# Reordering the routing stretch ahead of the expert loop in a two-layer SSM, Fourier and mixture-of-experts kernel

## Chip, cores and metric

One core of one Trainium2 chip. The metric is the device time of one execution in microseconds (us), given as the median of several runs.

## What is computed

Two layers over 256 image tokens and 256 context tokens of width 1024. Each layer normalises and modulates the tokens, mixes them (a bidirectional state-space scan and a 2-D Fourier mix, both gated), adds and normalises, and then applies a mixture of experts. The change touches only what stands at the head of the mixture of experts:

```python
def _moe(h, router_w, router_bias, w1, w3, w2, ws1, ws3, ws2):   # h: 512 tokens in layer 0, 256 in layer 1
    scores = jax.nn.sigmoid(h @ router_w)                        # 64 experts in 8 groups
    sel = scores + router_bias                                   # best 4 groups by their two best, then
    top_e = lax.top_k(sel, TOP_K)[1]                             # the 8 best experts of each token
    gate = take(scores, top_e); gate = gate / gate.sum() * 2.5
    ...                                                          # tokens sorted into blocks of one expert
    def body(acc, blk):
        tok, g, e = blk
        xb = h_pad[tok]
        hb = jax.nn.silu(xb @ w1[e]) * (xb @ w3[e])
        return acc.at[tok].add((hb @ w2[e]) * g[:, None]), None
    shared = (jax.nn.silu(h @ ws1) * (h @ ws3)) @ ws2            # one expert for all tokens
    return routed[:n_tok] + shared
```

## The kernel before

Everything is written out by hand for five engines, each with its own instruction list, tied by counting semaphores. All is f32. `l` is the layer (0 or 1) and `nt` its number of 128-token tiles: 4 in layer 0, 2 in layer 1. Each layer runs in three parts: the token mixer, the routing stretch, and the expert loop.

**The routing stretch.** For each tile, TensorE transposes the normalised tokens (`u2_transposes`, L959), ScalarE scales and copies them into `u2T` (L1352), and TensorE then forms the router's logits (`logits`, L970) and transposes the tokens back (L973); ScalarE takes the sigmoid (L1359) and copies the tokens for storing (L1361). The next tile's logits wait for both copies. In layer 0 the rows for the final gate (`g2_rows`, L1024) stand in between for the first two tiles. VectorE routes two tiles at a time (`route`, L1758 to L1787). Then TensorE counts the tokens of each expert (`count_tokens`, L1031 to L1034, psum bank 7). From the count VectorE makes the plan (`plan_steps`, L1806 on; `expert_list`, up to L1842; `place_experts`; `expert_row`, L1845 and L1847, which marks `blocks_ready`; `place_tokens`, L1872 to L1896).

Then `one_hot(i)` writes two lists for each tile: `onec` (the column of each slot, 128x512, L1901) and `onep` (its place in the block, 128x1024, L1903). GpSimd multiplies `onec` by the token's number (L2038). TensorE sums products of both (`slot_table`, L1047, 16 instructions a tile), ScalarE copies the sum (L1390), TensorE folds it (L1050), and VectorE's `slot_table` (L1919 to L1922) makes the tables of token numbers (`tblg`). `gates(i)` (L1908 to L1914) forms the eight gates of each token of tile i from `scores`; it is needed only after the loop.

**Shared work.** The shared expert is computed in the same stretch, in pieces: `shared_up(i)` (16 instructions of L980 for two tiles, so 8 for each), ScalarE's silu (L1367), VectorE's product (`shared_h`, L1792), two transposes (`shared_ht`, L986 and L987), VectorE's copy (`shared_ht`, L1796), `shared_down(i)` (eight instructions of L992) and ScalarE's copy (`shared_out`, L1373). Its weights lie in the buffers of the third expert, so SyncE may load that expert only when the last `shared_down` has ended (L583).

**The expert loop.** Each step takes three experts' weights, 3 MB each: two experts share a pair of half-filled blocks, block 0, and one fills block 1 alone. GpSimd gathers the tokens of a block from DRAM (`gather`, index copy L2056, indirect DMA L2060) into one of two buffers `xg`. TensorE transposes them (`x_transpose`, L1091), ScalarE (L1401) and VectorE (L1962) copy one half each, and TensorE runs `pair_up` (32 instructions of L1105) or `alone_up` (L980), the transposes, `pair_down` (L1134) or `alone_down` (L992). SyncE loads the next pair's up weights when `pair_up` is done (semaphore `up`, L587), and the down weights after the down products (L590).

**What starts the loop.** SyncE, GpSimd and the others wait for `blocks_ready` and read the number of steps from it. At the start SyncE loads the first pair (6 MB), then, after the last shared product, the third expert; in layer 0 it then issues the small parameters of layer 1 and two 2 MB pieces of its modulation weights, the second one when VectorE has copied the first token block (L474). The gathers wait for `tblg`, for the stored tokens, and for the semaphore `xt_tp`: gather i waits for i + 2, and TensorE adds 3 to it once when the token buffers are free. `x_transpose(0)` waits for the gather, for ScalarE's mark `xt_act` and for VectorE's mark `xt_dve`; VectorE gives its own after all of `gates`.

## Time and profile before

| | us |
|---|---|
| median of 3 runs | 2822.78 |
| lowest and highest run | 2819.46, 2827.2 |
| the profiled execution's own time | 2817.16 |
| its span, first to last instruction | 2815.2 |
| TensorE matmuls busy | 2556.5 (91%) |
| VectorE busy | 962.3 (34%) |
| ScalarE busy | 543.5 (19%) |
| GpSimd busy | 250.2 (9%) |
| mean of the DMA engines over the span | 264 GB/s |

The page cuts the span into 40 slices of 70 us. Three of its lines show the stages; each digit is a share in tenths:

```profile
PE   6999999999987999899999889999996899999994
...
PEclk8999999999999999999999989999998899999997
DMA  8764444444426999999999844764451799999983
```

The first 770 us are layer 0's mixer, the two stretches of nines in the DMA line are the two expert loops (about 910 to 1550 us and 2215 to 2750 us), and the short stretch before each is where tokens are routed. Times below are us from the span's start. The timelines name the source line of an instruction and, in brackets, how long its engine had been idle before it and what released it. PE is TensorE, DVE is VectorE, ACT is ScalarE, POOL is GpSimd, SPq is SyncE's DMA queue.

### The profile page before, as it was taken

The numbers are of one execution on the slowest core, as the hardware profiler recorded it, in microseconds if no ns is written. First come the engines' busy times: TensorE is split into PE (matmuls) and PEld (weight loads), VectorE is DVE, ScalarE is ACT, GpSimd is POOL, SyncE is SP. The second block draws the span as 40 slices with busy tenths as digits, with TensorE's granted clock in tenths as the row PEclk, the third lists the DMA queues.
The fourth block names the chain that finished last, engine by engine and source line by source line (L and its number), as shares of the span: only waits on it lengthen the run. The fifth ranks groups of instructions, "written<-read, shape, count | busy, mean of one in ns | idle before, by whom it ended". The sixth has DMA issues, their size and how long they took to land. (4 is left out here: it accounts for less than half of the span.)

```text
span 2815.2 us, 35251 instructions
## 1 busy us (share of the span) xinstructions
PE 2556.5 (91%) x11348; PEld 1622.4 (58%) x11348; DVE 962.3 (34%) x2249; ACT 543.5 (19%) x1210; POOL 250.2 (9%) x400
## 2 busy tenths in 40 slices
PE   6999999999987999899999889999996899999994
PEld 3878888787873343343333377878884333433431
DVE  1336624448165111111111474445616211111114
ACT  1223411334121111111111022224311111111110
POOL 0000000000002111111111000000000112111110
PEclk8999999999999999999999989999998899999997
DMA  8764444444426999999999844764451799999983
GB/s 291 243 203 153 150 144 140 135 150 146 150 83 234 407 406 410 410 403 398 410 410 380 323 136 124 239 198 144 141 165 63 312 398 391 392 399 390 382 354 139
DMA packets 293119, 742.43 MB, mean 264 GB/s; under 512 B 33176, under 2 KB 208416, under 8 KB 238240
## 3 DMA queue, kind: packets, MB, share of 16 engines
q1 hardware_dynamic: 264672, 665.59, 63.3%
q0 software_dynamic: 28352, 75.56, 6.9%
q8 instruction: 61, 1.00, 0.1%
q14 instruction: 34, 0.28, 0.0%
HBM read 734.60 MB, written 52.58 MB: 280 GB/s over the span
## 5 line engine op out<-in xcount | busy, mean ns | idle before, releaser
L747 PE MATMUL psum<-arena 128*128 128x256 f32 x1984 | 450.1, 386 | 8.9 <-ACT arena L1202 5.0
L1105 PE MATMUL psum<-arena 128*64 128x512 f32 x1472 | 360.8, 635 | 83.0 <-DMA arena<-in_w 83.0
L747 PEld LDWEIGHTS psum<-arena 128*128 128x128 f32 x1984 | 381.6, 194 | 65.6 <-issue 5.7
L980 PE MATMUL psum<-arena 128*128 128x512 f32 x832 | 375.3, 595 | 0.0
L1982 DVE COPY arena<-psum 128x512 f32<-128x512 f32 x92 | 63.6, 691 | 614.5 <-PE psum L992 310.3
L1105 PEld LDWEIGHTS psum<-arena 128*64 128x64 f32 x1472 | 112.4, 145 | 265.4 <-issue 259.8
L1418 ACT ACTIVATE arena<-psum 128x512 f32<-128x512 f32 x92 | 55.0, 598 | 1054.2 <-PE psum L992 591.9
L980 PEld LDWEIGHTS psum<-arena 128*128 128x128 f32 x832 | 152.4, 192 | 155.3 <-issue 155.3
L758 PE MATMUL psum<-arena 128*128 128x256 f32 (+1 forms) x1088 | 236.1, 375 | 5.0 <-ACT arena L1202 5.0
L758 PEld LDWEIGHTS psum<-arena 128*128 128x128 f32 x1088 | 202.4, 197 | 37.3 <-ACT arena L1202 5.2
L992 PE MATMUL psum<-arena 128*128 128x512 f32 x416 | 197.8, 619 | 5.8 <-DVE arena L1796 3.6
L1545 DVE SCALAR_TENSOR_TENSOR grow<-psum,par,grow 128x255 f32<-128x255 f32 (+1 forms) x304 | 136.1, 479 | 149.6 <-ACT grow L1261 144.0
L2082 POOL DMA_INDIRECT results<-arena,ids x92 | 92.8, 1008 | 920.5 <-DVE arena L1982 920.5
L907 PE MATMUL psum<-arena 128*128 128x256 f32 x768 | 173.2, 379 | 0.0
L1134 PE MATMUL psum<-arena 128*64 128x512 f32 x736 | 168.1, 599 | 0.0
L1979 DVE COPY arena<-psum 128x256 f32<-128x256 f32 x92 | 39.0, 424 | 369.0 <-PE psum L987 369.0
L907 PEld LDWEIGHTS psum<-arena 128*128 128x128 f32 x768 | 144.1, 190 | 23.0
L992 PEld LDWEIGHTS psum<-arena 128*128 128x128 f32 x416 | 76.8, 195 | 120.8 <-issue 115.5
L1091 PEld LDWEIGHTS psum<-cst,arena 128*128 128x128 f32 x736 | 94.9, 194 | 81.7 <-issue 57.5
L2032 POOL MEMSET arena<- 128x1024 f32 x4 | 3.7, 950 | 1371.1 <-DVE arena L1787 1371.1
L1091 PE MATMUL psum<-cst,arena 128*128 128x128 f32 x736 | 105.5, 288 | 21.7 <-DMA arena<-tokens,idg 20.9
L1134 PEld LDWEIGHTS psum<-arena 128*64 128x64 f32 x736 | 48.7, 136 | 113.8 <-issue 113.8
(305 smaller groups left out, 2476.9 us busy)
## 6 DMA issues: line engine op xcount, KB each, us to landing
arena<-in_w SPq DMA_DIRECT2D x414, 1024.0 KB, 14.7
arena<-in_w_in SPq DMA_DIRECT2D x92, 1024.0 KB, 5.2
arena<-in_w_ada SPq DMA_DIRECT2D x32, 1024.0 KB, 7.9
arena<-results POOLq DMA_DIRECT2D x12, 2048.0 KB, 9.5
arena<-in_w_br_ssm SPq DMA_DIRECT2D x24, 768.0 KB, 4.5
arena<-in_w_ada SPq DMA_DIRECT2D x8, 2048.0 KB, 15.2
arena<-cumulated SPq DMA_DIRECT2D x36, 384.0 KB, 4.2
arena<-in_w_br_four SPq DMA_DIRECT2D x12, 1024.0 KB, 5.2
```

The source lines that it names most:

```text
L747: last = mm(o[:, a, :], w[:, k, a * P:(a + 1) * P], rhs[:, k, :], start=k == 0, stop=k == ks - 1, skip_group_check=True)
L758: last = mm(o[:, a, 0:cols], lhs[:, k, a * P:(a + 1) * P], w[:, k, 0:cols], start=k == 0, stop=k == KD - 1, skip_group_check=True)
L907: last = mm(o[:, a, :], w[:, k, a * P:(a + 1) * P], rhs[:, k, :], start=k == 0, stop=k == KD - 1, skip_group_check=True)
L980: last = mm(o.rearrange("p (a n) -> p a n", a=2), lhs(k), w[:, k, :, :], start=k == 0, stop=k == KD - 1)
L992: last = mm(bank[5 + half][:, :], src[:, k, :], w[:, k, half * 512:(half + 1) * 512], start=k == 0, stop=k == 1)
L1091: last = tp(psum[:, 2 + k // 4, (k % 4) * P:(k % 4 + 1) * P], xg[b].rearrange("p (q k) -> p k q", k=KD)[:, k, :], ident)
L1105: last = mm(bank[0][c, :].rearrange("p (a n) -> p a n", a=2), xTe[0][:, k, c], w13[b][:, k, :, :], start=k == 0, stop=k == KD - 1)
L1134: last = mm(bank[5 + half][c, :], hT[0][:, k, c], w2s[b][:, k, half * 512:(half + 1) * 512], start=k == 0, stop=k == 1)
L1418: a_(ysb[b][:, 0:512], bank[5], ACT.Copy).then_inc(z["y_act"], 1)
L1545: i_ = V.scalar_tensor_tensor(dst, src[:, a * SEQ + lo + sh:a * SEQ + hi + sh], par[:, 60 + tap * 20 + ch:61 + tap * 20 + ch], dst, ALU.mu ...
L1982: V.tensor_copy(ysb[b][:, 512:1024], bank[6]).then_inc(z["y_dve"], 1)
L2082: gp.indirect_dma_start(scratch["y"][l], bass.IndirectOffsetOnAxis(ap=ids[:, q:q + 1], axis=0), ysb[b], None, bounds_check=last_row, oob_i ...
```

## The change

It keeps every computation and moves pieces of it.

- TensorE adds 3 to `xt_tp` right after the first two tiles (layer 0) or after both (layer 1), no longer after the last `shared_out`.
- In layer 0 the third tile's logits and the fourth tile's transposes stand in the middle of `shared_up(0)`; `shared_up(1)` is ahead of the count; `slot_table` is ahead of `shared_down(2)` and `shared_ht(3)`.
- In layer 1 the count stands in the middle of `shared_up(0)`, and `shared_ht(0)`, `shared_down(0)` and `shared_ht(1)` come after `experts_to_row`.
- VectorE multiplies `onec` by the token numbers itself, and GpSimd's four (two) multiplications and their semaphore `columns_numbered` go. In layer 0 `one_hot(0)` and `(1)` come ahead of `shared_h(2)`, and `one_hot(2)` and `(3)` ahead of `shared_h(3)`. In layer 1 the two `shared_h` and the first `shared_ht` move behind `place_experts`, the second one behind the lists.
- VectorE's `slot_table` comes ahead of all `gates` in layer 0; in layer 1 `gates(0)` stays ahead of it.
- ScalarE copies the table's sum ahead of `shared_out(2)`.
- The second block's first `x_transpose` stands in the middle of the first `pair_up`.

```diff
--- before.py
+++ after.py
@@ -386,7 +386,7 @@
         t_gr = stage("gate_rows_ready", 1, 0)
 
         names = ("u2_normed u2_transposed u2_ready logits routed counted placed rank_tp blocks_ready "
-                 "back_tp back_copied u2_stored0 u2_stored1 u2_stored2 u2_stored3 onehots columns_numbered table_sum table_copied table_folded "
+                 "back_tp back_copied u2_stored0 u2_stored1 u2_stored2 u2_stored3 onehots table_sum table_copied table_folded "
                  "router_in shared_in shared_up shared_sil shared_h shared_ht shared_htc shared_y shared_out "
                  "g2_diag g2_rows g2_ready scores").split()
 
@@ -993,13 +993,13 @@
                     return last
 
 
-                def shared_up(i):
+                def shared_up(i, between=None):
                     if i == 0:
                         pe.wait_ge(s["shared_in"], of(l, "shared_in", 48))
                         pe.wait_ge(s["g2_ready"], of(l, "g2_ready", nt // 2))
                     if i >= 2:
                         pe.wait_ge(s["shared_h"], of(l, "shared_h", i - 1))
-                    up(bank[i % 2], lambda k: u2T[:, k, i * P:(i + 1) * P], w13[2]).then_inc(s["shared_up"], 1)
+                    up(bank[i % 2], lambda k: u2T[:, k, i * P:(i + 1) * P], w13[2], between).then_inc(s["shared_up"], 1)
 
                 def shared_ht(i):
                     pe.wait_ge(s["shared_h"], of(l, "shared_h", i + 1))
@@ -1041,7 +1041,6 @@
                 def slot_table():
                     for i in range(nt):
                         pe.wait_ge(s["onehots"], of(l, "onehots", 2 * i + 2))
-                        pe.wait_ge(s["columns_numbered"], of(l, "columns_numbered", i + 1))
                         for j in range(TOPK):
                             c = slice(j % 2 * HALF, (j % 2 + 1) * HALF)
                             last = mm(bank[7][c, 0:P], onec[i][:, j, :], onep[i][:, j, :], start=i == 0 and j < 2, stop=i == nt - 1 and j >= 6)
@@ -1051,16 +1050,23 @@
 
                 if nt == 2:
                     g2_rows(0)
-                for i in range(nt):
+                for i in range(2):
                     u2_transposes(i)
-                    if nt == 4 and i < 2:
+                    if nt == 4:
                         g2_rows(i)
                     logits(i)
-                shared_up(0)
-                count_tokens()
-                shared_up(1)
-                shared_ht(0)
+                pe.sem_inc(z["xt_tp"], 3)
                 if nt == 4:
+                    def third_tile():
+                        logits(2)
+                        u2_transposes(3)
+
+                    u2_transposes(2)
+                    shared_up(0, third_tile)
+                    logits(3)
+                    shared_up(1)
+                    count_tokens()
+                    shared_ht(0)
                     shared_down(0)
                     shared_ht(1)
                     experts_to_row()
@@ -1068,17 +1074,22 @@
                     shared_up(2)
                     shared_up(3)
                     shared_ht(2)
+                    slot_table()
+                    shared_down(2)
+                    shared_ht(3)
                 else:
+                    shared_up(0, count_tokens)
+                    shared_up(1)
                     experts_to_row()
-                shared_down(nt - 2)
-                shared_ht(nt - 1)
-                slot_table()
+                    shared_ht(0)
+                    shared_down(0)
+                    shared_ht(1)
+                    slot_table()
                 shared_down(nt - 1)
 
                 pe.wait_ge(s["shared_out"], of(l, "shared_out", nt))
                 pe.sem_inc(z["down"], 3)
                 pe.sem_inc(z["up"], 2)
-                pe.sem_inc(z["xt_tp"], 3)
                 pe.sem_inc(z["ht_tp"], 2)
                 pe.wait_ge(s["blocks_ready"], of(l, "blocks_ready", 1))
                 n = pe.value_load(bexp[0:1, P:P + 1], min_val=1, max_val=STEPS)
@@ -1141,8 +1152,7 @@
                     down(hT[1], w2s[2]).then_inc(z["down"], 1)
 
                 x_transpose(0, 0, 1)
-                x_transpose(1, 1, 1)
-                pair_up(0, 1)
+                pair_up(0, 1, lambda: x_transpose(1, 1, 1))
                 with pe.Fori(0, STEPS // UNR) as ii:
                     for u in range(UNR):
                         i = ii * UNR + u
@@ -1385,9 +1395,12 @@
                     shared_out(1)
                     shared_silu(2)
                     shared_silu(3)
-                shared_out(nt - 2)
+                else:
+                    shared_out(0)
                 act.wait_ge(s["table_sum"], of(l, "table_sum", 1))
                 a_(tabT, bank[7][:, 0:P], ACT.Copy).then_inc(s["table_copied"], 1)
+                if nt == 4:
+                    shared_out(2)
                 shared_out(nt - 1)
                 act.wait_ge(s["g2_ready"], of(l, "g2_ready", nt // 2))
                 act.sem_inc(z["xt_act"], 1)
@@ -1898,8 +1911,10 @@
                 def one_hot(i):
                     if i == 0:
                         dve.wait_ge(s["g2_ready"], of(l, "g2_ready", nt // 2))
-                    V.tensor_tensor(onec[i], cst[:, C_STEP:C_STEP + HALF].unsqueeze(1).to_broadcast([P, TOPK, HALF]),
-                                    slotc[:, i, :].unsqueeze(2).to_broadcast([P, TOPK, HALF]), ALU.is_equal).then_inc(s["onehots"], 1)
+                    link(V.tensor_tensor(onec[i], cst[:, C_STEP:C_STEP + HALF].unsqueeze(1).to_broadcast([P, TOPK, HALF]),
+                                         slotc[:, i, :].unsqueeze(2).to_broadcast([P, TOPK, HALF]), ALU.is_equal))
+                    V.tensor_tensor(onec[i], onec[i], cst[:, C_TOK + i * TOPK:C_TOK + (i + 1) * TOPK].unsqueeze(2).to_broadcast([P, TOPK, HALF]),
+                                    ALU.mult).then_inc(s["onehots"], 1)
                     V.tensor_tensor(onep[i], cst[:, C_STEP:C_STEP + P].unsqueeze(1).to_broadcast([P, TOPK, P]),
                                     slotp[:, i, :].unsqueeze(2).to_broadcast([P, TOPK, P]), ALU.is_equal).then_inc(s["onehots"], 1)
 
@@ -1923,32 +1938,39 @@
 
                 for q in range(nt // 2):
                     route(q)
-                shared_h(0)
+                if nt == 4:
+                    shared_h(0)
                 plan_steps()
                 expert_list()
-                shared_h(1)
-                shared_ht(0)
-                place_experts()
                 if nt == 4:
+                    shared_h(1)
+                    shared_ht(0)
+                    place_experts()
                     shared_ht(1)
-                expert_row()
-                if nt == 2:
-                    shared_ht(1)
+                    expert_row()
+                else:
+                    place_experts()
+                    shared_h(0)
+                    expert_row()
+                    shared_h(1)
+                    shared_ht(0)
                 place_tokens()
-                if nt == 4:
-                    shared_h(2)
                 one_hot(0)
                 one_hot(1)
                 if nt == 4:
+                    shared_h(2)
+                    one_hot(2)
+                    one_hot(3)
                     shared_h(3)
                     shared_ht(2)
-                    one_hot(2)
-                    one_hot(3)
+                else:
+                    shared_ht(1)
+                    gates(0)
+                slot_table()
+                if nt == 4:
+                    gates(0)
                     shared_ht(3)
-                for i in range(nt // 2):
-                    gates(i)
-                slot_table()
-                for i in range(nt // 2, nt):
+                for i in range(1, nt):
                     gates(i)
                 dve.sem_inc(z["xt_dve"], 1)
                 dve.sem_inc(z["y_dve"], 1)
@@ -2033,10 +2055,6 @@
                 link(last)
                 for b in range(2):
                     gp.dma_start(first[:, b:b + 1], sent[:, b:b + 1]).then_inc(e_s[l][b], 16)
-                for i in range(nt):
-                    gp.wait_ge(s["onehots"], of(l, "onehots", 2 * i + 1))
-                    G.tensor_tensor(onec[i], onec[i], cst[:, C_TOK + i * TOPK:C_TOK + (i + 1) * TOPK].unsqueeze(2).to_broadcast([P, TOPK, HALF]),
-                                    ALU.mult).then_inc(s["columns_numbered"], 1)
                 gp.wait_ge(s["blocks_ready"], of(l, "blocks_ready", 1))
                 for i in range(nt):
                     gp.wait_ge(s[f"u2_stored{i}"], of(l, f"u2_stored{i}", 16))
```

## Rows read from the trace of the kernel before

**Rows 1.** Busy time by window, layer 0's loop: engines, clock, DMA share, GB/s

```profile
910.00:1010.00 100.00, 90.48 (x327) 37.49 (x328) 15.00 (x28) 10.30 (x21) 17.92 (x30) 0.93 1.00 411
```

**Rows 2.** Timeline of TensorE, layer 0: start, us, line, instructions [idle before <-releaser]

```profile
806.41 2.00 PE L970 MATMUL psum<-arena 128*128 128x64 f32 x16 [1.25 <-ACT arena L1352]
...
822.94 3.68 PE L970 MATMUL psum<-arena 128*128 128x64 f32 x16 [3.00 <-ACT arena L1352]
...
828.11 7.82 PE L980 MATMUL psum<-arena 128*128 128x512 f32 x16
...
848.31 3.70 PE L992 MATMUL psum<-arena 128*128 128x512 f32 x8 [2.16 <-DVE arena L1796]
...
875.75 3.71 PE L1047 MATMUL psum<-arena 128*64 128x128 f32 x64
...
893.49 1.97 PE L1091 MATMUL psum<-cst,arena 128*128 128x128 f32 x8 [9.73 <-DMA arena<-tokens,idg]
...
899.74 7.88 PE L1105 MATMUL psum<-arena 128*64 128x512 f32 x32
```

**Rows 3.** The chain that ended last, in order of time, layer 1: start, us, what

```profile
2195.45 6.39 DMA arena<-tokens,idg
...
2206.68 8.05 PE psum L1105 x32
```

**Rows 4.** Timeline of GpSimd, layer 0, then layer 1

```profile
886.13 1.11 POOL L2060 DMA_INDIRECT arena<-tokens,idg  x1 [1.97 <-PEq L1081]
...
2179.84 1.95 POOL L2038 TENSOR_TENSOR arena<-arena,cst 128x512 f32<-128x512 f32 x1 [19.43 <-DVE arena L1901]
...
2195.45 1.12 POOL L2060 DMA_INDIRECT arena<-tokens,idg  x1 [6.21 <-PEq L1081]
```

**Rows 5.** Timeline of VectorE, layer 0

```profile
816.45 0.81 DVE L1452 TENSOR_SCALAR arena<-xres,mv,rsq 128x1024 f32<-128x1024 f32 x1
...
827.01 0.29 DVE L1758 TENSOR_TENSOR arena<-arena 128x128 f32<-128x128 f32 x1 [2.98 <-ACT arena L1359]
...
839.04 0.22 DVE L1806 TENSOR_SCALAR arena<-psum 128x64 f32<-128x64 f32 x1 [2.17 <-PE psum L1034]
...
853.16 0.42 DVE L1872 TENSOR_SCALAR arena<-psum 128x256 f32<-128x256 f32 x1
...
864.28 0.42 DVE L1792 TENSOR_TENSOR arena<-arena,psum 128x256 f32<-128x256 f32 x1 [2.80 <-ACT arena L1367]
...
865.22 1.22 DVE L1903 TENSOR_TENSOR arena<-cst,arena 128x1024 f32<-128x1024 f32 x1
...
882.57 0.22 DVE L1919 TENSOR_SCALAR arena<-psum 128x64 f32<-128x64 f32 x1
...
888.82 0.24 DVE L1914 TENSOR_SCALAR arena<-arena 128x8 f32<-128x8 f32 x1
```

**Rows 6.** Timeline of TensorE, layer 1

```profile
2151.42 8.35 PE L980 MATMUL psum<-arena 128*128 128x512 f32 x16
...
2181.93 1.97 PE L1047 MATMUL psum<-arena 128*64 128x128 f32 x16 [8.91 <-POOL arena L2038]
...
2187.34 5.78 PE L992 MATMUL psum<-arena 128*128 128x512 f32 x8
```

**Rows 7.** Timeline of SyncE's DMA queue, layer 0: start, us, line, issues

```profile
884.51 0.81 SPq L587 DMA_DIRECT2D arena<-in_w  x2
```

**Rows 8.** Timeline of VectorE, layer 1

```profile
2156.92 0.23 DVE L1787 TENSOR_SCALAR arena<-arena 128x128 f32<-128x128 f32 x1
...
2160.86 0.22 DVE L1806 TENSOR_SCALAR arena<-psum 128x64 f32<-128x64 f32 x1 [0.15 <-PE psum L1034]
...
2187.65 0.22 DVE L1919 TENSOR_SCALAR arena<-psum 128x64 f32<-128x64 f32 x1 [0.63 <-PE psum L1050]
```

**Rows 9.** GpSimd's gathers in layer 1: wait after the index copy, time to landing

```profile
  POOL idg L2056: 25.4, 32
...
DMA to landing us min/median/max: 4.3/9.2/10.7
```

## Prediction

> **What bounds the kernel now.** I read the page's busy table and slices first, then windows over the loops, then the timelines of each engine in the stretches ahead of them. TensorE is busy 91% of the span, yet in the two stretches in which the expert steps run, the DMA engines are the resource that is full: the first 100 us of layer 0's loop show DMA share 1.00 and 411 GB/s, with TensorE at 90 of 100 us [rows 1]; layer 1's loop is alike. A step there waits for the next pair's weights. What is asked of those loops is fixed in bytes, so their end moves with their start. The start is the end of the first pair_up: only then may SyncE load the next pair. So I read the routing stretch ahead of each loop, engine by engine, from the last projection to the first pair_up (899.74 + 7.88 = 907.6 in layer 0, 2206.68 + 8.05 = 2214.7 in layer 1) [rows 2, 3], and asked which wait ends last at each link.
>
> The chain is: logits, routing on VectorE, count on TensorE, plan, place_tokens, the one-hot lists, slot_table, the two gathers, x_transpose, pair_up. In layer 1 the first gather stands 6.21 us on TensorE's mark of free token buffers (L1081), which comes after the last shared work; in layer 0 the same wait is 1.97 us, because the table itself is late [rows 4]. In layer 0 VectorE reaches slot_table at 882.57, with no idle before it: TensorE's table products ended at 875.75 + 3.71 = 879.46, and two gate blocks stood between [rows 2, 5].
>
> **Layer 0, part by part.** (Before, then after, in us of this execution.)
>
> *Second half of the token tiles.* Now TensorE waits 3.0 us for each tile's copy, and the logits run at half clock: 3.68 against 2.00 for the same 16 matmuls [rows 2]. The change puts half of shared_up(0) (eight matmuls, half of about 7.0 us at full clock, from the row of 7.82 that begins slow) into each of the two gaps. The last tile is normalised at 816.45 + 0.81 = 817.3 whatever is done [rows 5], so: transpose to 818.4, half of shared_up to 821.9, logits to 823.9. Route 1 starts at 824.1, when route 0 has just ended, instead of 827.01 [rows 5]. shared_up(1), 7.0 us, moves ahead of the count and ends at 831.8, later than route 1 (831.0), so it costs the count 0.8 us. From the count's start to the plan it is 839.04 less the end of shared_up(0), 835.9, some 3.2 [rows 2, 5]; plan starts at 835.1: 3.9 us gained. The bounds are 0 (half clock as now) and 3.9; I take 3.9, since nothing longer than the 1.25 us wait ahead of the fast row [rows 2] is left in this stretch.
>
> *What that takes away.* shared_up(1) used to cover TensorE while VectorE planned; now TensorE is idle from about 835 to 844 and shared_down(0) starts cold. After 8.9 us idle in layer 1, the table products took 1.97 for 16 (0.93 at layer 0's 3.71 for 64) and the eight matmuls of a shared_down 5.78 against 3.70 [rows 2, 6]. shared_down(0) is on the path (VectorE waits behind it for shared_ht(1) and the expert row). Bounds 0 and 3.5 us; I take 2.8. place_tokens then starts at 852.0 against 853.16 [rows 5].
>
> *Lists.* place_tokens is 8.3 us; after it VectorE now waits 2.80 for the third silu [rows 5]. With one_hot(0) and (1) ahead of it that stall goes: the lists begin at 860.3 against 864.6. Four one-hots now have their multiplication on VectorE. The 1024-wide list takes 1.22, so I take 0.61 to 0.7 for each 512-wide operation, 2.5 us a tile in all [rows 5]; the bounds of the new operation are 0.61, half of that row, and 1.95, GpSimd's row for the same operation [rows 4]. With two small products the lists end at 870.7. TensorE's table products overlap all but the last quarter and end at 873.7 (5.8 earlier). slot_table no longer stands behind gate blocks: VectorE starts it at 874.5 against 882.57, 8.1 us earlier. The gather follows at 876.9 against 886.13.
>
> *What is late next.* x_transpose(0) also needs VectorE's own mark (xt_dve), which stands behind all gate blocks. Table and two gate blocks take 882.57 to 889.06, so a gate block is 2.8 [rows 5]; table, four blocks and one copy end at 887.1. TensorE's last shared product ends near 882 and its copy at 883.3, the gathers land by 884 and 889. So x_transpose(0) starts at 887.1 against 893.49, with cold clock again. From there to the end of pair_up it was 14.1 us, 2.4 of them a wait for the second gather; with the second transpose inside the pair 12.9 us: pair_up ends at 900.0 against 907.6, 7.6 earlier. Second, the DMA: from the third expert's load at 884.51 [rows 7] to 907.6 the engines had little idle time, and that load waits for the last shared_down, only 1.5 us earlier (883.0). Its 2.1 MB, 4.2 MB of modulation and 1 MB of later gathers are 7.4 MB, 18 us at 411 GB/s: busy to 901. So some 1.5 us of the 7.6 is given back. Layer 0: **6 us**; bounds 1.5 and 8.5 (shared_down warm).
>
> **Layer 1.** The count stands inside shared_up(0): its first half, half cold, runs from 2151.42 to 2156.2 [rows 6], the route ends at 2156.92 + 0.23, and from the count's start to the plan it is 1.1 to 1.3 (2160.86 less the end of shared_up(0), 2159.77) [rows 6, 8], so plan starts at 2158.5 against 2160.86, 2.4 earlier. shared_up(1) then ends at 2168.9, ahead of when VectorE needs the expert row (2169.2). Two small products move behind place_experts, all of them ready. That takes 0.4 more off, since VectorE no longer waits for a transpose. The lists are then done at 2181.3: before, the second one ended with its GpSimd product, 1.95 long as the first [rows 4], at 2184.4. Table products, copy and fold take 3.1. gates(0) ahead of slot_table costs nothing, as it ends at 2184.45 in that shadow. slot_table starts 2184.45 against 2187.65 [rows 8], 3.2 earlier. The gather needs no mark behind shared work any more. Before, it was issued 7.8 after slot_table's start, 6.21 of that the wait; with the 0.8 that always lies between index copy and gather (25.4 us for 32) [rows 4, 9] it is 2.4: 2186.8 against 2195.45. shared_down(1) ends at 2190.1 (cold, 5.78), its copy 2191.2, so TensorE is there first. The gather lands 6.4 after issue as in the chain [rows 3]; the least in this layer is 4.3, the median under load 9.2 [rows 9]. I take 6.4, the nearest: 2193.2 against 2201.89. Then 12.9 us for transpose, copy, half pair, transpose, half pair; it is 12.8 now. What the mid-pair transpose saves is TensorE's wait for a copy (0.9), what it can cost is a wait for the second gather inside the pair; its data come at about 2198, needed at 2201. pair_up ends 2206.1 against 2214.7. The DMA engines are nearly idle ahead of that, so nothing is given back. Layer 1: **8.6 us**; bounds 5.8 (a landing of 9.2) and 11 (landing 4.3, and the clock stays high).
>
> *A rule that speaks against it.* GpSimd's first gather now falls beside gate blocks, products with two SBUF inputs. So far the gather beside gates(3) took 1.11 us of GpSimd and the one with VectorE idle 1.12 [rows 4], which shows no hold in the issue; the landings are 7.4 and 6.4 [rows 2, 3, 4]. The Trainium skill, "SBUF — State Buffer", section "SBUF: two separate sides", says VectorE can hold the port that GpSimd writes descriptors through, so that the transfer starts only when VectorE lets go; rival 1 is what that would make.
>
> *Edits taken at nothing.* ScalarE copies the table sum ahead of shared_out(2): it has no work then, and shared_out(2) is wanted only by the next shared_down. In layer 1 shared_ht(0) and shared_down(0) stand behind the expert row on TensorE; their readers on VectorE come later still. GpSimd's clearing of the token buffers, begun when the first route is done, now runs beside route 1 of layer 0 instead of in a gap; the count has 0.8 us to spare there, so it costs 0 to 1. The four multiplications that leave GpSimd leave nothing behind them there. Queued behind the new waits inside shared_up(0) is only its own second half. SyncE's queue keeps its order; its second modulation load waits for the first token copy, which comes 6 us earlier.
>
> **Sum.** 6 + 8.6 = 14.6 off the 2817.16 us of the profiled execution (span 2815.2): 2802.6. The median of the runs is 2822.78, 5.6 above it; the loss should be the same: **2808**.
>
> **Rivals.**
> 1. *The gather is held behind the gates.* Before, gates(3) ended at 889.06 and the gather landed 4.4 later, just the 4.3 of the shortest landing [rows 2, 5, 9]; the traffic of the third expert explains 7.3 as well. Held until 887.1, it lands at 891.5 and the pair ends at 904.4: layer 0 gives 3.2, in all 11.8, 2811. Chance 0.12.
> 2. *Layer 0's start is the DMA's.* If the load stream from the third expert on decides alone, layer 0 gives 1.5: 10.1, 2812.7. For it: little idle; against: the third expert's load must wait for buffers anyhow. Chance 0.12.
> 3. *shared_down(0) warm.* Layer 0 gives 8.5 and layer 1 10: 2804. Chance 0.1.
> 4. *Slower: the half clock.* The clock was full at 806.41 and half at 822.94, after waits of 3 us [rows 2]. If it is low from 812 through both halves, logits, shared_up(1) and the count, plan comes at 854 (15.3 later than now), and the rest keeps its 2.1 gain: layer 0 loses 13.2, layer 1 gives 8.6: +4.6, 2827. It decides once plan is over 14.6 us later than I forecast, nearly all of the stretch at half clock. Against it: even behind that slow stretch shared_up(0) took only 7.82, some 1.6 us of it at half clock [rows 2]. Chance 0.05.
> 5. *The mark isn't what holds GpSimd* (a store of tokens, or the sequencer): layer 1's 8.6 shrinks to 3.2: 2813.6. Chance 0.04.
>
> **How the numbers follow.** The forecast has 0.57. What a measurement of this kernel can tell is about 0.3%, 8.5 us, so faster is below 2814.3. The runs before spread from 2819.46 to 2827.2, some 3 us about the middle. Of the forecast and rival 3 a tenth falls above 2814.3 by that and by the bounds (0.60 of 0.67 is left); rivals 1, 2 and 5 lie just inside, and a third or more of them falls out (0.17 of 0.28). Faster 0.77, same 0.17, slower 0.06. Range 2799 to 2820: all cases but the slower one, with that spread at both ends.
>
> **What would show it.** Plan of layer 0 (L1806) 3 to 4 us earlier; the first L992 at 5.8 to 7.2 us, after 9 us idle; no 2.80 wait ahead of one_hot; gather-to-table distance under 2.5 us in both layers; GpSimd without elementwise work; first L1091 of layer 0 waiting for VectorE's last L1914, not for the gather; loops of the same length as now. A loop that is longer by the gain, or a first L1091 of layer 0 waiting for a gather issued ten us before, would prove me wrong.

## The result, and the profile after

| | before | changed |
|---|---|---|
| median, first comparison | 2821.46 us (2819.46 to 2827.2, 4 runs) | 2807.18 us (2800.67 to 2810.88, 4 runs) |
| ratio, 95% interval | | 0.9939 (0.9922 to 0.9956) |
| median, second comparison | 2824.04 us (23 runs) | 2808.02 us (6 runs) |
| ratio, 95% interval | | 0.9939 (0.9915 to 0.9963) |
| span of the profiled execution | 2815.2 us | 2806.5 us |

The change takes 14 to 16 us off. 2808 was forecast, 14.6 less than before.

The two profiled spans differ by only 8.7 us, and a comparison of their clock times would mislead: the changed kernel arrives at the routing stretch 8.1 us later (803.65 against 795.59), with nothing changed ahead of it. So everything below is counted from the first token transposes of a layer's routing stretch (the first instruction of `u2_transposes`, "T" below). A line such as "T + 104.0" can then be compared between kernels. T is 795.59 and 2131.65 in the trace of before, 803.65 and 2135.38 in that of the changed kernel.

TensorE in layer 0, changed kernel (start us, us, line, instructions [idle before <-releaser]), beside [rows 2]:

```profile
819.65 3.67 PE L980 MATMUL psum<-arena 128*128 128x512 f32 x8
823.15 1.89 PE L970 MATMUL psum<-arena 128*128 128x64 f32 x16
...
852.09 6.29 PE L992 MATMUL psum<-arena 128*128 128x512 f32 x8 [9.04 <-DVE arena L1809]
...
863.09 13.90 PE L980 MATMUL psum<-arena 128*128 128x512 f32 x32
...
877.15 3.71 PE L1046 MATMUL psum<-arena 128*64 128x128 f32 x64
...
894.50 1.70 PE L1102 MATMUL psum<-cst,arena 128*128 128x128 f32 x8 [4.46 <-DVEq L1975]
```

L980 x8 is the first half of shared_up(0), in the third tile's gap, which was some 3.0 us idle like the fourth's, and the logits behind it take 1.89 where they took 3.68. L992 at 852.09 is the first shared_down: 9.04 us of idle ahead of it and 6.29 long, cold. L1046 are the 64 table products; TensorE comes to them straight from 13.90 us of shared_up. The first transposes at 894.50 wait for VectorE's mark (DVEq), no longer for a gather.

VectorE in layer 0, beside [rows 5]:

```profile
842.83 0.23 DVE L1819 TENSOR_SCALAR arena<-psum 128x64 f32<-128x64 f32 x1 [3.15 <-PE psum L1034]
...
859.53 0.42 DVE L1885 TENSOR_SCALAR arena<-psum 128x256 f32<-128x256 f32 x1
...
867.87 0.69 DVE L1914 TENSOR_TENSOR arena<-cst,arena 128x512 f32<-128x512 f32 x1
868.60 0.69 DVE L1916 TENSOR_TENSOR arena<-arena,cst 128x512 f32<-128x512 f32 x1
869.21 1.22 DVE L1918 TENSOR_TENSOR arena<-cst,arena 128x1024 f32<-128x1024 f32 x1
870.35 0.68 DVE L1914 TENSOR_TENSOR arena<-cst,arena 128x512 f32<-128x512 f32 x1
...
881.71 0.22 DVE L1934 TENSOR_SCALAR arena<-psum 128x64 f32<-128x64 f32 x1 [2.90 <-PE psum L1049]
...
894.06 0.23 DVE L1929 TENSOR_SCALAR arena<-arena 128x8 f32<-128x8 f32 x1
```

Plan at 842.83, place_tokens at 859.53, lists from 867.87, slot_table at 881.71, the last gate block's end at 894.29. One tile's lists run from 867.87 to 870.35, 2.48 us with the multiplication (L1916, 0.69), and nothing stands between place_tokens and the lists. The last list ends at 878.15, after the table products have begun.

GpSimd's first gather in layer 0, and both in layer 1, beside [rows 4]:

```profile
884.17 1.07 POOL L2078 DMA_INDIRECT arena<-tokens,idg  x1 [0.87 <-POOL idg L2074]
...
2190.74 1.07 POOL L2078 DMA_INDIRECT arena<-tokens,idg  x1 [0.83 <-POOL idg L2074]
...
2195.14 1.05 POOL L2078 DMA_INDIRECT arena<-tokens,idg  x1 [3.12 <-issue]
```

GpSimd no longer waits for TensorE's mark ahead of either layer's first gather; 0.83 to 0.87 is the usual distance behind the index copy. SyncE's load of the third expert in layer 0, beside [rows 7]:

```profile
890.79 0.81 SPq L587 DMA_DIRECT2D arena<-in_w  x2
```

TensorE in layer 1, beside [rows 3, 6], and VectorE's plan and slot_table there, beside [rows 8]:

```profile
2196.11 1.13 PE L1102 MATMUL psum<-cst,arena 128*128 128x128 f32 x8 [2.50 <-issue]
2198.07 3.65 PE L1116 MATMUL psum<-arena 128*64 128x512 f32 x16 [0.83 <-ACT arena L1414]
2203.37 1.15 PE L1102 MATMUL psum<-cst,arena 128*128 128x128 f32 x8 [1.64 <-DMA arena<-tokens,idg]
```

```profile
2162.31 0.23 DVE L1819 TENSOR_SCALAR arena<-psum 128x64 f32<-128x64 f32 x1 [1.49 <-PE psum L1034]
...
2188.33 0.23 DVE L1934 TENSOR_SCALAR arena<-psum 128x64 f32<-128x64 f32 x1 [0.17 <-PE psum L1049]
```

The first transposes are at 2196.11, the half pair behind them at full clock (3.65 for 16), and then TensorE waits 1.64 us in the middle of the pair, for the second gather. The first transposes do not wait for the first gather any more, but for the last shared product and its copy by ScalarE:

```profile
2193.66 1.02 ACT L1383 ACTIVATE arena<-psum 128x1024 f32<-128x1024 f32 x1 [6.18 <-PE psum L992]
```

In all eleven traces with the early mark they start 2.30 to 2.45 us after the start of this copy, and the profile names no gather in ten of them. In the six of them in which the profile gives the first gather's landing, it is 3.3 to 4.1 us after its issue and 0.5 to 1.8 ahead of the transposes.

**Where the time went.** Each kernel's trace, cut at the same points. "Pair" is the end of the first pair_up, "loop" runs from there to the start of the last eight alone_down matmuls, all in us:

| kernel | start to T | layer 0: T to pair | loop 0 | layer 1: T to pair | loop 1 | rest |
|---|---|---|---|---|---|---|
| before | 795.6 | 112.0 | 651.4 | 83.1 | 536.7 | 63.8 |
| before, again | 803.0 | 114.1 | 651.1 | 83.2 | 536.8 | 63.6 |
| changed | 803.6 | 104.0 | 655.1 | 72.7 | 538.0 | 60.4 |
| changed, again | 801.2 | 102.2 | 656.8 | 72.0 | 537.4 | 60.4 |
| mark_alone | 801.9 | 111.2 | 653.1 | 81.5 | 536.5 | 61.9 |
| mark_late | 797.6 | 108.5 | 652.2 | 79.6 | 536.6 | 63.2 |
| no_mid_pair | 802.6 | 103.6 | 655.0 | 78.7 | 536.8 | 62.3 |
| mark_alone_gathers_first | 797.0 | 107.5 | 661.6 | 77.6 | 536.1 | 62.1 |
| plan_covered | 797.6 | 99.9 | 656.0 | 72.6 | 536.3 | 62.1 |
| plan_covered_gates_late | 803.3 | 97.7 | 657.6 | 72.5 | 536.8 | 63.7 |
| one_load_less_owed | 804.5 | 104.0 | 651.5 | 72.3 | 536.6 | 62.2 |
| lists_on_gpsimd | 797.3 | 103.9 | 655.6 | 72.6 | 538.1 | 62.2 |
| covered_and_less_owed | 799.1 | 99.9 | 650.3 | 72.3 | 537.3 | 63.5 |
| all_three | 805.2 | 97.7 | 651.1 | 72.5 | 536.4 | 63.6 |

Start to T and rest are stretches in which nothing was changed. The part between the loops, up to layer 1's T, is 572.3 to 575.0 in all of them (569.0 in mark_late). The two traces of each kernel give, for layer 0 with its loop, 763.4 and 765.2 before, 759.1 and 759.0 changed: 5 us less, of which the stretch alone is 8 to 12 and the loop gives 4 to 6 back. For layer 1 with its loop, 619.8 and 620.0 before, 610.7 and 609.4 changed: 10 us less, all of it in the stretch. The rest behind the second loop is 60.4 in both traces of the changed kernel and 63.7 before, but 62.1 to 63.7 in kernels whose code there is the changed kernel's; these 3 us were not looked into and are not counted as the change's.

### The profile page after: what moved, and what is told of

Its sections match the earlier page's. It is cut to its first block and busy times, and to the rows that moved or that the text cites. A ratio compares the mean times of both kernels' runs of the same rounds, so it can differ in the third digit from the quotient of the medians.

```text
span 2806.5 us, 35244 instructions
## 1 busy us (share of the span) xinstructions
PE 2563.5 (91%) x11348; PEld 1623.7 (58%) x11348; DVE 962.5 (34%) x2255; ACT 543.0 (19%) x1210; POOL 238.5 (8%) x394
## 3 DMA queue, kind: packets, MB, share of 16 engines
q1 hardware_dynamic: 264672, 665.59, 63.7%
## 5 line engine op out<-in xcount | busy, mean ns | idle before, releaser
L1116 PE MATMUL psum<-arena 128*64 128x512 f32 x1472 | 367.9, 645 | 83.6 <-DMA arena<-in_w 80.6
L980 PE MATMUL psum<-arena 128*128 128x512 f32 x832 | 374.8, 594 | 0.0
L2004 DVE COPY arena<-psum 128x512 f32<-128x512 f32 x92 | 63.6, 691 | 612.8 <-PE psum L992 308.7
L980 PEld LDWEIGHTS psum<-arena 128*128 128x128 f32 x832 | 152.2, 192 | 154.3 <-issue 154.3
L992 PE MATMUL psum<-arena 128*128 128x512 f32 x416 | 198.5, 621 | 12.9 <-DVE arena L1809 9.7
L1145 PE MATMUL psum<-arena 128*64 128x512 f32 x736 | 168.1, 599 | 0.0
L992 PEld LDWEIGHTS psum<-arena 128*128 128x128 f32 x416 | 77.2, 195 | 128.2 <-issue 115.9
## 6 DMA issues: line engine op xcount, KB each, us to landing
arena<-in_w SPq DMA_DIRECT2D x414, 1024.0 KB, 14.6
```

The lines of the kernel that those rows point to most:

```text
L980: last = mm(o.rearrange("p (a n) -> p a n", a=2), lhs(k), w[:, k, :, :], start=k == 0, stop=k == KD - 1)
L992: last = mm(bank[5 + half][:, :], src[:, k, :], w[:, k, half * 512:(half + 1) * 512], start=k == 0, stop=k == 1)
L1116: last = mm(bank[0][c, :].rearrange("p (a n) -> p a n", a=2), xTe[0][:, k, c], w13[b][:, k, :, :], start=k == 0, stop=k == KD - 1)
L1145: last = mm(bank[5 + half][c, :], hT[0][:, k, c], w2s[b][:, k, half * 512:(half + 1) * 512], start=k == 0, stop=k == 1)
L2004: V.tensor_copy(ysb[b][:, 512:1024], bank[6]).then_inc(z["y_dve"], 1)
```

## Experiments

**again_before** and **again_after** are the two kernels unchanged.

> The kernel before, unchanged, for a second trace. In the first pair of traces the changed kernel reached the first transposes of layer 0's routing stretch at 803.65 us and the kernel before at 795.59, although nothing ahead of that point differs. If that is chance, this trace has some other value between about 790 and 805. If the order of the instructions later in the program had an effect on it, it is again near 795.6. From there to the end of the first pair_up it should again be 112.0 us in layer 0 and 83.1 in layer 1, within 0.5.

> The changed kernel again. My theory: the routing stretch is 104.0 us in layer 0 (8.0 shorter) and 72.7 in layer 1 (10.4 shorter), to within 0.5, since nothing in it is left to chance but the gathers' landing; layer 0's loop gives some 2 to 4 us back, since the DMA engines still owe part of the modulation weights when it begins. In all some 14 us, ratio 0.995. The rival, that the loops' length is chance of several us and nothing is given back, has layer 0's loop at 656.7 plus or minus 2 here.

The start to T was 803.0 in the second trace of before: it is chance, and over all traces it lies between 795.6 and 805.2 with the same instructions. Layer 0's stretch came 2.1 longer than in the first, not within 0.5 (the plan already stands at T + 45.4 against 43.5, and the third tile's first transposes take 1.73 us where they took 1.04); layer 1's is the same to 0.1. The changed kernel gave 102.2 and 72.0 (layer 0 off by 1.8), and loop 0 was 656.8, 5.4 to 5.7 longer than before and so above the 2 to 4 that I expected. The rival as I wrote it, 656.7 plus or minus 2, holds that number too, so this run does not decide between them. What speaks against chance is the table as a whole: 651.1 and 651.4 before, 655.0 and more in every kernel with the whole reordering and all its loads (one_load_less_owed, below, takes it up). Of the 1.8, 1.1 lies in the first shared_down of the second trace:

```profile
849.38 5.22 PE L992 MATMUL psum<-arena 128*128 128x512 f32 x8 [9.03 <-DVE arena L1809]
```

It took 5.22, against 6.29 in the first: after 9 us idle the clock comes back at a different point of it. In the other four kernels with these 9 us of idle it took 5.22, 6.17, 6.18 and 6.26.

**mark_alone**: the kernel before, and only the mark moved.

```diff
                     logits(i)
+                    if i == 1:
+                        pe.sem_inc(z["xt_tp"], 3)
                 shared_up(0)
...
                 pe.sem_inc(z["up"], 2)
-                pe.sem_inc(z["xt_tp"], 3)
```

> The kernel before, with one edit: TensorE marks the token buffers free after the second tile instead of after the last shared product. My theory (the mark holds GpSimd 6.2 us in layer 1 and 2.0 in layer 0, the table is what is late in layer 0): layer 1's stretch 83.1 to about 77 (6.2 shorter), layer 0's 112.0 to about 110; in all 7 to 8 us, ratio 0.997. The rival that the mark isn't what holds GpSimd: no change in either stretch, ratio 1.000. The rival that the mark is all of the change's worth: 18 us off the two stretches.

Measured: 2823.78 us against 2824.04, ratio 0.9995 (0.9981 to 1.0009): nothing. My expectation of 7 to 8 us failed. The mark did what I said: T to the first transposes of layer 1 fell from 70.2 to 63.5, 6.8 less. But T to the end of the pair fell only from 83.1 to 81.5. TensorE, then GpSimd, then SyncE's queue, in layer 1:

```profile
2201.94 1.13 PE L1092 MATMUL psum<-cst,arena 128*128 128x128 f32 x8 [2.34 <-issue]
2208.91 1.97 PE L1092 MATMUL psum<-cst,arena 128*128 128x128 f32 x8 [5.84 <-DMA arena<-tokens,idg]
2210.81 9.13 PE L1106 MATMUL psum<-arena 128*64 128x512 f32 x32
...
2196.75 1.12 POOL L2061 DMA_INDIRECT arena<-tokens,idg  x1 [0.84 <-POOL idg L2057]
...
2201.19 1.05 POOL L2061 DMA_INDIRECT arena<-tokens,idg  x1 [3.13 <-issue]
...
2200.36 21.85 SPq L587 DMA_DIRECT2D arena<-in_w  x6
```

The first gather is now issued at 2196.75, ahead of the third expert's load (2200.36), the second one at 2201.19, just behind it. TensorE waits 5.84 us for it; in the kernel before, the second gather went 6.0 us behind the load, and landed after 4.3. A wait was traded for another. In layer 0 the stretch is 111.2 (expected 110): the first gather is issued 1.1 us earlier, at T + 89.5, but the transposes still start at T + 97.8, and loop 0 is some 2 us longer. I had noticed neither in the prediction nor here that the first gather's gain does not carry the second one with it.

**mark_alone_gathers_first** tests that cause: mark_alone, and the third expert's load also waits for the second gather.

```diff
                 sp.wait_ge(s["shared_y"], of(l, "shared_y", nt))
+                sp.wait_ge(e_g[l][1], 16)
                 up_in(expert_of(0, 2), 2)
```

> The kernel with the mark alone, and SyncE now also waits for the first landing of the second block's gather before it loads the third expert. Theory: the mark's 6.8 us were eaten in layer 1 because the second gather (issued at 2201.19, 7.7 us to land) shared the DMA engines with that load (issued at 2200.36). With the load behind it the gather lands 4.3 to 4.6 after issue, and from the first transposes to the end of pair_up it is 13 to 15 us instead of 18.0: stretch 76 to 78.5 against 81.5. The rival, that the second gather is late by itself (GpSimd's 3.1 us ahead of it, or its own descriptors): still about 81.5. In layer 0 the load waits some 8 us more, and the loop there may get 2 to 5 us longer, so the total may well stay.

```profile
2204.02 1.13 PE L1093 MATMUL psum<-cst,arena 128*128 128x128 f32 x8 [2.34 <-issue]
2207.79 1.97 PE L1093 MATMUL psum<-cst,arena 128*128 128x128 f32 x8 [2.65 <-DMA arena<-tokens,idg]
...
2203.38 1.05 POOL L2062 DMA_INDIRECT arena<-tokens,idg  x1 [3.13 <-issue]
```

Measured: with the load behind the gather, the second gather, issued at 2203.38, lets the transposes go at 2207.79, 4.4 later, where it was 7.7 before. The stretch is 77.6, inside the 76 to 78.5 expected; the rival (81.5) falls. In layer 0, too, the first transposes then start 4.3 us after the first gather's issue, where it was 8.4, and the stretch is 3.7 shorter than in mark_alone (107.5). The price is where it was expected too: loop 0 is 661.6, over 8 us longer than in mark_alone, more than the 2 to 5 I allowed, and the ratio is 1.0 (0.9987 to 1.0014).

**mark_late**: the changed kernel with the mark at its old place, behind the last shared copy.

```diff
                     logits(i)
-                pe.sem_inc(z["xt_tp"], 3)
...
                 pe.sem_inc(z["up"], 2)
+                pe.sem_inc(z["xt_tp"], 3)
```

> The changed kernel, with the mark put back behind the last shared product. My theory: in layer 0 the last shared copy ends at 891.1 in the changed kernel's trace, so the first gather goes at about 892.4 instead of 884.2 and lands at 899: the stretch is 104.0 + 4 to 5 = 108 to 109. In layer 1 the copy ends at 2194.7, the gather goes at 2196 instead of 2190.7: 72.7 + 5 to 6 = 78. So about 9 us of the 18 are the mark's here, 9 the reordering's. The rival that only the reordering counts: 104.0 and 72.7 stay.

```profile
885.00 1.45 POOL L2078 DMA_INDIRECT arena<-tokens,idg  x1 [9.11 <-PEq L1092]
...
2187.83 1.07 POOL L2078 DMA_INDIRECT arena<-tokens,idg  x1 [5.67 <-PEq L1092]
```

Measured: ratio 0.9977 (0.9964 to 0.999), 2817.91 us. GpSimd waits 9.11 us in layer 0 and 5.67 in layer 1 for the mark. Layer 0's stretch is 108.5 (expected 108 to 109), layer 1's 79.6 (expected 78): 5.4 and 7.2 longer than with the mark, and loop 0 is 2.9 to 4.6 shorter, so that more than half of the first is given back. So beside the reordering the mark is worth some 10 us (2817.9 against 2808.0), and alone it was worth nothing.

**no_mid_pair**: the changed kernel with the second block's transposes ahead of the first pair_up.

```diff
-                pair_up(0, 1, lambda: x_transpose(1, 1, 1))
+                x_transpose(1, 1, 1)
+                pair_up(0, 1)
```

> The changed kernel, with the second block's transposes ahead of the first pair_up again. Theory, from the run with the mark alone: the second gather is queued behind the third expert's load (8.2 us to land in layer 1), and the mid-pair place hides that wait behind half a pair. In the changed kernel's trace it landed when the second transposes began, at 2203.4; without the cover pair_up begins only at 2204.5 and ends at 2211.8 to 2213.5 against 2208.1: layer 1's stretch 72.4 + 3.6 to 5.4, 76 to 78. In layer 0 that gather is there in time, so 0 to 0.8 longer. The rival that the mid-pair place saves just the wait for a copy: 0.9 in either layer.

```profile
2194.78 1.13 PE L1102 MATMUL psum<-cst,arena 128*128 128x128 f32 x8 [2.35 <-issue]
2201.91 1.97 PE L1102 MATMUL psum<-cst,arena 128*128 128x128 f32 x8 [6.00 <-DMA arena<-tokens,idg]
2203.81 9.04 PE L1116 MATMUL psum<-arena 128*64 128x512 f32 x32
```

Measured: 0.996 (0.9945 to 0.9975), 2813.44 us. In layer 1 TensorE waits 6.00 us for the second gather with nothing to do, then runs the transposes and a pair that begins cold (9.04): stretch 78.7, 6.3 longer than 72.4 and a little over the 3.6 to 5.4 expected. Layer 0 is unchanged (103.6). The rival, 0.9 in each, falls. Without the mid-pair place the early mark hardly pays in layer 1: 78.7, against 79.6 with the late mark and the mid-pair place. The same late landing is in the changed kernel,

```profile
DMA to landing us min/median/max: 8.2/8.2/8.2
```

(8.2 us for the second gather of layer 1; 7.1 in its second trace, 7.9 in no_mid_pair), but half a pair lies over it, and the second half then runs at full clock (3.65).

**plan_covered**: shared_up(2) of layer 0 fills TensorE's idle time while VectorE plans.

```diff
                     count_tokens()
                     shared_ht(0)
+                    shared_up(2)
                     shared_down(0)
...
                     shared_down(1)
-                    shared_up(2)
                     shared_up(3)
```

> The changed kernel, with shared_up(2) of layer 0 moved to directly behind the count and shared_ht(0), where TensorE is idle for 9.0 us while VectorE plans. Theory: shared_down(0), which starts cold now (6.29 and 5.22 us in two traces), takes 3.7; place_tokens 1.5 to 2.6 us earlier; TensorE is no longer busy with 14 us of shared_up when the lists are ready, so the table is 3 to 4 us earlier; the marks follow. Layer 0's stretch 103.1 to 99 to 100.5; layer 1's 72.4 unchanged. How much is left at the end tests the other point: if the loads still owed at the loop's start set layer 0's loop, it gets 1 to 3 us longer for it. The rival (a cold start costs nothing there, VectorE is the bound): stretch within 0.5 of 103.1.

```profile
846.06 3.70 PE L992 MATMUL psum<-arena 128*128 128x512 f32 x8 [2.18 <-DVE arena L1809]
...
865.30 5.39 PE L1046 MATMUL psum<-arena 128*64 128x128 f32 x64
...
884.33 1.23 PE L1102 MATMUL psum<-cst,arena 128*128 128x128 f32 x8 [4.46 <-DVEq L1975]
```

Measured: 0.9926 (0.9908 to 0.9945), 2803.48 us. The shared_down behind 2.18 us of idle takes 3.70. T to pair is 99.9, 3.2 less than the 103.1 of the changed kernel's two traces; the rival falls. The edit does two things, and the trace parts them. Against the changed kernel's first trace, whose plan also starts at T + 39.2, place_tokens comes 2.6 us earlier (T + 53.3 against 55.9): this is the cold shared_down, which is on the path. slot_table comes 4.1 earlier (T + 73.9 against 78.1); the other 1.5 come from TensorE, which is no longer in shared_up when the lists are ready: the table products begin at T + 67.7 and end at T + 73.1, 1.2 behind the last list, where in the changed kernel they begin only at T + 73.5. Loop 0 is 656.0, as in the changed kernel, and not 1 to 3 longer as I expected: the third expert's load is issued 4.1 us earlier as well (T + 83.0 against 87.1).

**plan_covered_gates_late**: VectorE's mark after the first gate block.

```diff
-                    sp.wait_ge(e[l]["xt_dve"], 2)
+                    sp.wait_ge(e[l]["xt_dve"], 3)
                     modulation(1, 1)
...
                     gates(0)
                     shared_ht(3)
-                for i in range(1, nt):
-                    gates(i)
                 dve.sem_inc(z["xt_dve"], 1)
...
+                gates(1)
+                gates(2)
                 x_copy(0, 0)
+                gates(3)
                 x_copy(1, 1)
```

> As the kernel with the plan covered, and in layer 0 VectorE gives its mark after the first gate block: gates 1 and 2 stand ahead of its first token copy, gates 3 ahead of the second one; SyncE's second modulation load waits for the second copy instead of the first. Theory: the first transposes wait for TensorE's last shared copy or the gather instead of VectorE's last gate block, 2 to 3 us earlier than with the plan covered alone; stretch of layer 0 about 97. The DMA engines owe the same bytes, 4 us later, so layer 0's loop gives back a good part: in total 0 to 2 us faster than with the plan covered alone. The rival that the loops' length is independent of what is owed at their start: 2 to 3 us faster in total.

Measured: 0.9931 (0.9915 to 0.9947), 2804.33 us, no better than plan_covered. The stretch is 2.2 shorter (97.7), the loop 1.6 longer (657.6). The third expert's load starts where it did (T + 83.0), so the shorter stretch leaves more to load. The edit also asks for the second modulation piece later, and how much of the 1.6 is due to that isn't shown.

**one_load_less_owed** asks why.

```diff
-                    sp.wait_ge(e[l]["xt_dve"], 2)
-                    modulation(1, 1)
...
-                    for j in range(2, ADA_WIDE[1]):
+                    for j in range(1, ADA_WIDE[1]):
                         modulation(1, j)
```

> The changed kernel, with the second 2 MB piece of layer 1's modulation weights loaded behind layer 0's expert loop instead of ahead of it. It tests why layer 0's loop is 4 to 5 us longer in every kernel whose stretch is shorter (655.0 to 657.6 against 651.1 and 651.4). Theory: the DMA engines still owe those bytes when the first pair_up ends. Without 2.1 MB (5.1 us at 411 GB/s) the loop is back at 651 to 652.5, the stretch stays at 103.1 within 1; what is behind the loop (572.7 to 574.8 to layer 1's first transposes) gets 0 to 5 longer, as the piece is waited for there. The rival (the loop's phases fall differently, whatever is owed): loop still at 655 to 657.

SyncE's queue at the end of layer 0's loop, and TensorE there:

```profile
1553.69 5.30 SPq L474 DMA_DIRECT2D arena<-in_w_ada  x3
...
1560.02 3.69 PE L990 MATMUL psum<-arena 128*128 128x512 f32 x8 [0.69 <-DVE arena L1999]
1569.65 6.24 PE L665 MATMUL psum<-arena,csil 128*32 128x512 f32 x32 [5.94 <-issue]
```

Measured: 0.9935 (0.9917 to 0.9952), 2805.27 us. Stretch 104.0, loop 0 651.5: the loop's extra 3.6 to 5.3 us are gone with 2.1 MB less to load, as expected, and the rival (655 to 657) falls. The three pieces behind the loop are issued from 1553.69, TensorE's first work on them (L665) starts at 1569.65, 9.6 us after the last alone_down began, as in the changed kernel, and the part between the loops is 572.8: the moved piece costs nothing there, the lower end of the 0 to 5 I allowed.

With this run the fourteen traces fall into line. What layer 0's loop takes goes with the time between the issue of the third expert's load and the end of the first pair_up, in which that load and the modulation pieces can pass (no run varied this time alone):

| load issued to pair's end | loop 0 | kernels |
|---|---|---|
| 22.3 to 23.2 us | 651.1 to 653.1 | before (2), mark_late, mark_alone |
| 16.4 to 16.9 | 655.0 to 656.8 | changed (2), no_mid_pair, lists_on_gpsimd, plan_covered |
| 14.7 | 657.6 | plan_covered_gates_late |
| 10.5 | 661.6 | mark_alone_gathers_first |
| 14.7 to 16.9, with 2.1 MB less | 650.3 to 651.5 | one_load_less_owed, covered_and_less_owed, all_three |

**lists_on_gpsimd**: the changed kernel with the multiplication on GpSimd again, under its old semaphore.

```diff
-                    link(V.tensor_tensor(onec[i], ..., ALU.is_equal))
-                    V.tensor_tensor(onec[i], onec[i], ..., ALU.mult).then_inc(s["onehots"], 1)
+                    V.tensor_tensor(onec[i], ..., ALU.is_equal).then_inc(s["onehots"], 1)
...
+                    G.tensor_tensor(onec[i], onec[i], ..., ALU.mult).then_inc(s["columns_numbered"], 1)
```

> The changed kernel, with the multiplication of the lists on GpSimd again. Theory: in layer 0 TensorE is busy until 877.2 in the changed kernel's trace, and only the last quarter of the table can wait for GpSimd's fourth product: 0 to 1 us. In layer 1 the second list is then waited for from GpSimd, about as late as it is from VectorE now (GpSimd 1.95 behind a VectorE list that is 0.7 earlier a tile): stretch 72.4 to 73.0. So this part of the change is worth under 1 us in each layer. The rival, that GpSimd's product is on the path in both layers with all of its 1.95: 2 us longer in each.

TensorE and GpSimd in layer 1:

```profile
2179.77 1.98 PE L1047 MATMUL psum<-arena 128*64 128x128 f32 x16 [0.61 <-POOL arena L2059]
...
2177.67 1.96 POOL L2059 TENSOR_TENSOR arena<-arena,cst 128x512 f32<-128x512 f32 x1 [0.63 <-DVE arena L1915]
```

Measured: 0.9945 (0.9925 to 0.9964), 2805.52 us; stretches 103.9 and 72.6. TensorE does wait for GpSimd's product (0.61), and slot_table of layer 1 starts 0.6 later than in the changed kernel, but the first transposes do not (T + 60.6 against 60.7 and 60.1), since they wait for the last shared copy. In layer 0 TensorE comes to the table from shared_up at T + 73.4 or 73.5 either way. Moving the multiplication to VectorE is worth nothing that can be seen. GpSimd's 1.95 us ran beside VectorE's lists, at a price: a 128x512 list on VectorE took 0.68 to 0.69 us alone and 1.20 to 1.53 beside GpSimd's product, in the kernel before and in this one. The other moves, the lists ahead of the silu products and slot_table ahead of the gates, were not taken back one by one, so their shares are read from the trace and not shown by a run.

**covered_and_less_owed** puts plan_covered and one_load_less_owed together, **all_three** also the late gates. Their edits are those above.

> The changed kernel with two edits together: shared_up(2) of layer 0 covers the plan, and the second modulation piece is loaded behind layer 0's loop. Theory: both savings stand, because the first shortens the stretch and the second takes away what the loop would give back: layer 0's stretch 99.9 to 100.5 (103.1 in the changed kernel), its loop 651 to 653 (655.1 and 656.8), everything else as in the changed kernel. In all 6 to 8 us under the changed kernel, ratio to the kernel before about 0.991. The rival that the loop takes back whatever the stretch gives: loop 654 or more, and no more than 4 us under the changed kernel.

Measured: 2798.9 us (2796.34 to 2800.05), ratio 0.9905 (0.9889 to 0.992). Stretch 99.9, loop 650.3. Both savings stand (the loop is a little under the 651 to 653 expected), and this is the fastest kernel of the study, 27 us under the kernel before and about 9 under the changed one.

> As the kernel before this one, and VectorE's mark in layer 0 after its first gate block, two gate blocks ahead of its first token copy and one ahead of the second. Theory: stretch 97.7 as in the run with late gates; the loads still owed (the third expert's and the first modulation piece, both behind the last shared product) now weigh more, so that loop is 652 to 654.5; 0.5 to 2 us faster in all than without this edit. The rival, that nothing is owed any more: loop 651.4 and 2.2 us faster.

Measured: 2800.02 us, 0.991 (0.9896 to 0.9923); stretch 97.7, loop 651.1. Between the expectation (loop 652 to 654.5) and the rival (651.4 and 2.2 us faster) the trace takes the rival's loop, but the runs show no gain over the kernel before this one. A difference of 2 us is less than these runs can tell, so it stays open.

## Why the prediction was right, point by point

Measured values are counted from T.

1. **The bound.** Right for the loops: layer 1's loop is 536.1 to 538.1 us in fourteen traces, whatever starts it, so its end moves with its start. For layer 0 it is right only with what is owed (point 6). Rival 2, that the load stream alone decides layer 0's start and it gives 1.5, falls: layer 0 gave 5.
2. **Second half of the tiles, layer 0.** Plan: T + 43.45 before, T + 39.18 after, 4.3 earlier; 3.9 was forecast. The clock did not fall in this part (1.89 for the logits). Rival 4 (half clock) falls.
3. **The cold shared_down.** 6.29 and 5.22 us, 2.6 and 1.5 above the 3.70 of full clock; 2.8 was taken. Rival 3 (warm) falls. place_tokens at T + 55.9 against 57.6, 1.7 earlier (forecast 1.2). plan_covered shows that it was rightly put on the path.
4. **Lists and table.** 2.48 a tile (2.5 forecast); slot_table T + 78.1 against 87.0, 8.9 earlier (8.1). The number is right, the step to it is not. With the lists done at 870.7, table products that overlap all but the last quarter (0.93 of 3.71) end at 871.6, and not at the 873.7 of the text. They ended at T + 77.2, 872.8 on that clock, because TensorE was in shared_up until T + 73.3 and ran all 64 behind it, while the last list was done at T + 74.5. So TensorE's shared work, not VectorE's lists, is late there, and plan_covered gains by it. The multiplication's cost was right, its worth was not asked: it is nil.
5. **What is late next.** Right: the first transposes wait for VectorE's last gate block, 7.1 us earlier than before (6.4), the pair ends 8.0 earlier (7.6) in the first pair of traces.
6. **The give-back in layer 0, mis-sized.** I took 1.5 us; the loop is 3.7 and 5.4 us longer. The mechanism was right (one_load_less_owed), the step that failed is "busy to 901": I let the DMA engines work without a hole from the third expert's load on. They did not, nor had they before ("little idle time" was 0.87, 0.62 and 0.92 busy in the three windows from 890 to 899). The sign that I had named, loops of the same length as now, failed for this loop, which gave back about half of what its stretch gained. Windows of the changed kernel (PE, PEld, DVE, ACT and POOL busy, clock, DMA share, GB/s):

```profile
890.00:893.00 3.00, 0.04 (x1) 0.00 (x0) 2.76 (x8) 1.02 (x1) 0.00 (x0) 1.00 0.46 100
893.00:896.00 3.00, 1.50 (x8) 1.32 (x8) 1.19 (x4) 0.00 (x0) 0.00 (x0) 0.81 0.98 410
896.00:899.00 3.00, 2.17 (x7) 0.84 (x8) 0.69 (x1) 0.60 (x1) 1.21 (x2) 0.50 0.69 237
899.00:902.00 3.00, 3.00 (x10) 0.89 (x9) 0.00 (x0) 0.00 (x0) 0.00 (x0) 0.55 0.63 198
902.00:905.00 3.00, 3.00 (x20) 1.50 (x18) 0.69 (x1) 0.60 (x1) 0.11 (x1) 1.00 1.04 378
```

Before 893 they are half idle (the load is issued at 890.79), and at 0.69 and 0.63 from 896 to 902; the second modulation piece is issued only at 896.9, after the first token copy. That this late issue makes the second hole is my reading of the trace, not tested by itself. The load came when forecast (T + 87.1, 882.7 on the prediction's clock, against 883.0), and so did the pair's end, so it is the holes, some 3 of the 17 us between, that leave bytes to the loop: by estimate 1.5 and 3, 4.5 in all, beside the 3.7 and 5.4 measured. That the stretch was 0.4 to 2.2 shorter than forecast hid part of this error: layer 0 gives 5 us, 6 was forecast.

7. **Layer 1.** Plan T + 26.9 against 29.2, 2.3 earlier (2.4); slot_table 3.1 earlier (3.2); gather T + 55.4 against 63.8, 8.4 earlier (8.6). The transposes began 5.4 after the gather's issue, not 6.4, and in the first trace they and both half pairs ran at full clock: the pair ends 10.3 earlier (8.6 forecast, bounds 5.8 and 11). In the second trace the first half was slow (5.35), and the pair ends 11 earlier all the same. Two steps were wrong. The forecast says that TensorE is there first and the gather comes last; it is the other way round. The gather landed 3.4 us after its issue in the changed kernel's second trace, and the transposes wait for the cold last shared_down and its copy, whose end was forecast at 2191.2 and came at 2191.0 on that clock, with 1.4 us from there to the transposes. And I had the second gather land at 2198 and be there in time. Counted the same way it came at about 2199.6, and TensorE waited 1.64 us for it, because the third expert's load is ahead of it. I had weighed the mid-pair place at 0.9; it is worth 6.3. That layer 1 still came within 1.5 us of its 8.6 is luck in part.
8. **Rival 1, the hold by the gates.** Falls. In layer 0 both gathers ran beside gate blocks without a pause; the second one, issued at 886.23, with gate blocks until 894.3:

```profile
DMA to landing us min/median/max: 4.6/4.6/4.6
```

That is 4.6 us; in the kernel before, the second gather of layer 1, issued at 2199.89 with VectorE idle, landed after 4.3. The Trainium skill, "SBUF — State Buffer", section "Who interferes with whom", says that in a probe products (`tensor_tensor`) and reductions did not stall a DMA of GpSimd's, and a copy did. The sentence I weighed in the prediction is about operations of the latter kind; the gate blocks that the gather ran beside are mostly of the former, and the trace agrees.

9. **Rival 5, the mark.** Falls as written: the mark does hold GpSimd (6.21 us, 0.84 once it is moved). What I had not drawn is that moving it alone gives nothing.
10. **The sum.** 6 + 8.6 = 14.6 was forecast; the traces give 5 + 10, the medians 14.3 and 16.0. The two terms were off by 1 and some 1.2 us in opposite directions. That the median of 2807.18 is within 1 us of 2808 is partly luck: between the two pairs of traces the stretches without a change differ by some 3 us each, one way (start to T) and the other (rest).

## What to carry to other kernels

A mark that is moved ahead frees only the first thing that waits for it: ask which transfer is issued right behind, and what else is now in front of it; the early mark paid here only once half a pair covered the second gather. Where a loop is bound by transfers, shorten its lead-in and look at what the engines still owe when it starts; a load that nobody needs yet belongs behind the loop. And count from a common point near the change: the same instructions ahead of it took 795.6 to 805.2 us.
